# A two-model kernel's prologue: activation table, token sums, a free PSUM bank, order of splits and of one load

## The chip, the cores and the metric

One core of a Trainium2 chip. The metric is the device time of one execution in microseconds (us), the median of several runs. The engines of the core: TensorE (PE: matmuls, PEld: its weight loads), VectorE (DVE), ScalarE (ACT), GpSimd (POOL), and SyncE (SP), which here only issues DMAs. Each engine runs its own program in order and meets the others at semaphores.

## The reference

Two models in a row on 256 tokens of width 1024, in float32. The first has two layers; each normalises x, projects it (pool, attention, indexer, memory attention, gates), lets an indexer pick 64 keys a token, attends to them with a relative bias, attends to 256 memory rows, and merges three gated branches. The second has one layer (a gated delta rule in both directions, a short convolution, a gated feed-forward). The part that matters here is the beginning:

```python
def rms_norm(x, g):
    x32 = x.astype(jnp.float32)
    y = x32 * lax.rsqrt(jnp.mean(x32 * x32, axis=-1, keepdims=True) + EPS)
    return (y * g.astype(jnp.float32)).astype(x.dtype)

# first layer
h = rms_norm(x, norm_g[l])
proj = h @ w_in[l]
mkv = rms_norm(mem, mem_norm_g[l]) @ w_mem_kv[l]
bias = rel_bias[rel_bucket(idx - qpos[None, :, None])]
```

## The kernel before

**Matmuls.** Everything is held with channels on partitions (xT is 128 x 8 x tokens). To keep float32 accuracy, both operands of a product are split into a high part (fp32r) and the low rest, and hi*hi + hi*lo + lo*hi are added in PSUM. The weights come as a stream of blocks of 512 KB (128 x 1024). SP loads block n into raw[slot n % 4] once DVE has split the block four places earlier (`lo_ready`, L422). ACT makes the high half (`split_hi`, L265: waits for the load and for the block four earlier to be done on PE), DVE the low half (`split_lo`, L272). PE then does 24 matmuls of 128 x 256 (`block_cols`, L292: 16 with the high half, 8 with the low), into stream_ps[slot], one PSUM bank a slot; it waits until that bank's last result has been evicted. `ahead(split, engine, G, s)` (L278) splits the block two places behind block s of group G. A group is four blocks.

**The prologue.** Group 0 (blocks 0 to 3) makes iqT and group 1 (blocks 4 to 7) qT of the first layer. They work on u = x * gain, not yet normalised, so that they needn't wait for the token norms; rstd is multiplied in as DVE evicts (`scaled`, L1023). `first_blocks` (L307) does blocks 0 and 1 in steps of one k as the parts of u arrive. Then comes the token sum: ACT squares xT (L571), POOL adds the eight squares (`add_squares`, L384, seven additions in place), PE multiplies by ones (L1620), ACT takes Ln and Exp (`rstd_of`, L369). Then blocks 2 to 7, then a product of rel_bias with a bucket table (L1637, into free_ps[1]) that ACT copies to rel_f (L604) and POOL writes out and reads back as hankel (L433, L435). Then the sums of mem's squares (L1641), and groups 2 to 5, which work on mem_hi and mem_lo of both layers (ACT L576, DVE L1050), their results scaled by mem_rstd. At L656 the first layer proper begins with group G0 + 2 on h_hi and h_lo; behind its first block stands the indexer's product (L1672 to L1679) with ikw_hi, made by ACT (L660) from wik.

**Order by hand.** Each engine's program is written out. ACT issues all loads of constants at its start (L553 to L562), ahead of its first activation. It issues the loads of wik and pool_w at L639 and L642, behind all evictions of the prologue. In ACT's program the two splits of `head` (L588, L589) come behind the squares, the splits of blocks 4 and 5 behind rstd_of, and the copy of rel_f (L604) ahead of the splits of group 2. In DVE's program, `head` (L1028) splits blocks 2 and 3 around evictions that wait for rstd. PE waits for cst before its first matmul (L1612).

Of the kernel before, what the change touches and what calls it, by code (L numbers as in the profile page):

```python
# [9 lines left out]
ACT = mybir.ActivationFunctionType  # L10
# [7 lines left out]
D = 1024  # L18
KT = D // P
S = 256  # L20
# [3 lines left out]
HEADS, HD = 8, 64  # L24
# [8 lines left out]
EPS = 1e-6  # L33
# [3 lines left out]
SLOTS = 4  # L37
# [41 lines left out]
def build(nc, a, out):  # L79

    with ExitStack() as ctx:
# [209 lines left out]

        def block_cols(pe, G, s, free, free_at, r_hi, r_lo, parts=None):  # L292


            pe.wait_ge(hi_ready, 4 * G + s + 1)
            pe.wait_ge(free, free_at)
            ps = stream_ps[s][:, 0:r_hi.shape[-1]]
            for k in range(KT):
                if parts and k % 4 == 0:
                    pe.wait_ge(parts[0], parts[1] + k // 4)  # L300
                with_hi(ps, w_hi[s][:, k, :], r_hi[:, k, :], r_lo[:, k, :], k == 0)
            pe.wait_ge(lo_ready, 4 * G + s + 1 + SLOTS)
            for k in range(KT):
                mm = nc.tensor.matmul(ps, w_lo[s][:, k, :], r_hi[:, k, :], start=False, stop=k == KT - 1)  # L304
            mm.then_inc(blk_done, 1)
# [109 lines left out]
        @block.sync  # L415
        def _(sp):

            first = 8 * LAYERS
            order = list(range(first, first + 8)) + list(range(0, first)) + list(range(first + 8, 4 * a["groups"] + AHEAD))
            for n, at in enumerate(order):  # L420
                s = n % SLOTS
                sp.wait_ge(lo_ready, n + 1)  # L422
                sp.dma_start(raw[:, s, :], a["stream"][at]).then_inc(w_in[s], 16)
            sp.wait_ge(stored, 32)

        @block.gpsimd
        def _(pool):
            nc.gpsimd.memset(eps_col[:, :], EPS).then_inc(consts_ready, 1)

# [121 lines left out]
        def _(act):  # L551
# [9 lines left out]
            act.dma_start(rel_sb[:, :], a["rel_bias"]).then_inc(rel_in, 16)  # L561
            act.dma_start(admit[:, :], a["admit"]).then_inc(admit_in, 16)  # L562
            act.wait_ge(gains_in, 16)
            for k in range(KT):
# [3 lines left out]
                if k in (1, 3):  # L568
                    split_hi(act, 0, k // 2)
            for k in range(KT):  # L570
                nc.scalar.activation(wideS[:, k, :], xS[:, k, :], ACT.Square).then_inc(sq_ready, 1)  # L571

# [20 lines left out]

            act.wait_ge(consts_ready, 1)
            head(0)
            for k in range(KT):
# [6 lines left out]
            act.wait_ge(relf_done, 1)  # L603
            nc.scalar.activation(rel_f[:, :], free_ps[1][0:HEADS, :], ACT.Copy).then_inc(relf_ready, 1)  # L604
            ahead(split_hi, act, 1, 2)
# [28 lines left out]
            for l in range(0, LAYERS):  # L634
                G = G0 + LAYER_GROUPS * l

                if l:
                    act.wait_ge(ikwlo_ready, l)
                act.dma_start(wik[:, :, :], a["wik"][l]).then_inc(wik_in, 16)  # L639
                if l:  # L640
                    act.wait_ge(mixed_done, 2 * l)
                act.dma_start(pool_w[:, :, :], a["pool_w"][l]).then_inc(poolw_in, 16)  # L642
                if l:
                    head(l)
                    for s in range(SLOTS):
                        ahead(split_hi, act, G + 1, s)
                        if s in (1, 3):
                            split_norm_half(l, s // 2)
# [364 lines left out]
        def _(dve):  # L1013
# [8 lines left out]

            def scaled(G, s, dst):  # L1023

                dve.wait_ge(blk_done, 4 * G + s + 1 + SLOTS)
                nc.vector.tensor_tensor(dst, stream_ps[s][:, 0:S], rstd[:, 0:S], ALU.mult).then_inc(dve_evac, 1)

# [31 lines left out]

            head(0)  # L1060
            for s in range(SLOTS):
                ahead(split_lo, dve, 1, s)
                if s in (1, 2):
                    split_mem_lo(0, s - 1)
                scaled(1, s, qT[:, s, :])
            for m in range(LAYERS):
# [543 lines left out]
        def _(pe):  # L1610
            pe.sem_inc(blk_done, SLOTS)
            pe.wait_ge(cst_in, 16)  # L1612

            def head(l):


                Gh, D = head_group(l), DVE_EVACS * l
                first_blocks(pe, Gh, dve_evac, D + 1, u_hi, u_lo, (ulo_ready, KT * l + 1), KT)
                pe.wait_ge(sqsum_ready, l + 1)
                nc.tensor.matmul(free_ps[0][:, 0:S], ones, wideS[:, 0, :], start=True, stop=True).then_inc(ss_ready, 1)  # L1620
                for s in range(AHEAD, SLOTS):
                    block_cols(pe, Gh, s, dve_evac, D + s + 1, u_hi, u_lo)
                for s in range(SLOTS):
                    block_cols(pe, Gh + 1, s, dve_evac, D + 4 + s + 1, u_hi, u_lo)

# [9 lines left out]
            head(0)  # L1635
            pe.wait_ge(rel_in, 32)
            nc.tensor.matmul(free_ps[1][0:HEADS, :], rel_sb[:, :], bucket_hot, start=True, stop=True).then_inc(relf_done, 1)  # L1637
            pe.wait_ge(memsum_ready, 1)
            pe.wait_ge(rstd_ready, 1)
            pe.wait_ge(relf_ready, 1)  # L1640
            nc.tensor.matmul(free_ps[0][:, 0:S], ones, mem_sq[:, 0, :], start=True, stop=True)  # L1641
# [541 lines left out]
```

## Time and profile before

| | |
|---|---|
| median of 3 runs | 1297.45 us (1296.86 to 1300.08) |
| profiled execution | 1302.77 us |
| its span | 1301.0 us |
| PE busy | 1227.4 us (94%) |
| DVE, ACT, POOL busy | 867.6, 632.5, 221.9 us |
| mean granted clock of PE | 0.98 |
| DMA | 196.34 MB, mean 151 GB/s |

The span runs from the first to the last instruction of one profiled execution. Busy time is the union of an engine's instructions; a wait is idle time in front of an instruction, put down to what ended last before it. The granted clock is 1.00 at 2.4 GHz and 0.50 at 1.2 GHz. Engine names with a q (ACTq) are the engine's sequencer, which issues DMAs.

### The profile page before, as it was taken

The numbers are of one execution on the slowest core, as the hardware profiler recorded it, in microseconds if no ns is written. First come the engines' busy times: TensorE is split into PE (matmuls) and PEld (weight loads), VectorE is DVE, ScalarE is ACT, GpSimd is POOL, SyncE is SP. The second block draws the span as 40 slices with busy tenths as digits, with TensorE's granted clock in tenths as the row PEclk, the third lists the DMA queues.
The fourth block names the chain that finished last, engine by engine and source line by source line (L and its number), as shares of the span: only waits on it lengthen the run. The fifth ranks groups of instructions, "written<-read, shape, count | busy, mean of one in ns | idle before, by whom it ended". The sixth has DMA issues, their size and how long they took to land.

```text
span 1301.0 us, 26912 instructions
## 1 busy us (share of the span) xinstructions
PE 1227.4 (94%) x11214; PEld 1187.6 (91%) x11214; DVE 867.6 (67%) x1385; ACT 632.5 (49%) x1022; POOL 221.9 (17%) x244
## 2 busy tenths in 40 slices
PE   5999999999999999998799899999999889999997
PEld 5898998999999989998699899999998889999997
DVE  4754855756868566574588686877877476855554
ACT  6644545543645445535477723333333545644443
POOL 3100150002100510021000062633733001000000
PEclk9999999999999999998899999999999899999999
DMA  6554564445655644455354333323233474566653
GB/s 247 182 166 155 170 188 130 130 140 169 215 168 165 188 141 140 130 167 171 97 173 154 116 103 99 96 85 115 71 94 99 146 224 149 179 194 183 190 195 113
DMA packets 59912, 196.34 MB, mean 151 GB/s; under 512 B 6382, under 2 KB 14088, under 8 KB 59664
## 3 DMA queue, kind: packets, MB, share of 16 engines
q1 hardware_dynamic: 49248, 179.33, 44.7%
q10 hardware_dynamic: 10016, 12.90, 2.9%
q0 software_dynamic: 528, 2.40, 0.7%
q8 instruction: 89, 1.46, 0.5%
q14 instruction: 31, 0.25, 0.1%
HBM read 190.37 MB, written 4.23 MB: 150 GB/s over the span
## 4 chain that ended last, share of the span: by engine, by line
PE 83%; DVE 6%; ACT 4%; issue 3%; DVEq 2%; POOLq 1%; DMA 0%; ACTq 0%
PE stream_ps L289 18%; PE stream_ps L290 17%; PE stream_ps L304 13%; PE stream_ps L283 4%; PE stream_ps L285 3%; PE stream_ps L284 3%; PE free_ps L1948 2%; PE free_ps L1960 2%; DVE w_lo L275 2%; PE stream_ps L1790 2%; PE stream_ps L2035 2%; ACT w_hi L269 1%; PE stream_ps L340 1%; PE stream_ps L345 1%; PE stream_ps L341 1%
## 5 line engine op out<-in xcount | busy, mean ns | idle before, releaser
L275 DVE TENSOR_TENSOR w_lo<-raw,w_hi 128x1024 fp32r<-128x1024 f32 x342 | 428.5, 1262 | 212.4 <-ACT w_hi L269 210.3
L269 ACT ACTIVATE w_hi<-raw 128x1024 fp32r<-128x1024 f32 x342 | 356.6, 1053 | 51.7 <-PE stream_ps L1790 26.2
L289 PE MATMUL stream_ps<-h_hi,w_hi 128*128 128x256 f32 (+1 forms) x1440 | 361.8, 289 | 14.1 <-DVE h_lo L1271 7.1
L290 PE MATMUL stream_ps<-h_lo,w_hi 128*128 128x256 f32 (+1 forms) x1440 | 355.8, 284 | 0.0
L289 PEld LDWEIGHTS stream_ps<-h_hi,w_hi 128*128 128x128 f32 x1440 | 274.6, 191 | 21.1 <-issue 14.6
L290 PEld LDWEIGHTS stream_ps<-h_lo,w_hi 128*128 128x128 f32 x1440 | 275.1, 191 | 0.2
L304 PE MATMUL stream_ps<-h_hi,w_lo 128*128 128x256 f32 (+1 forms) x1376 | 193.0, 283 | 3.0 <-DVE w_lo L275 3.0
L304 PEld LDWEIGHTS stream_ps<-h_hi,w_lo 128*128 128x128 f32 x1376 | 176.8, 189 | 3.4 <-DVE w_lo L275 3.4
L283 PE MATMUL stream_ps<-h_hi,w_hi 128*128 128x256 f32 (+1 forms) x384 | 116.7, 304 | 2.1 <-DVE w_lo L275 2.1
L285 PE MATMUL stream_ps<-h_hi,w_lo 128*128 128x256 f32 (+1 forms) x384 | 108.6, 283 | 0.0
L284 PE MATMUL stream_ps<-h_lo,w_hi 128*128 128x256 f32 (+1 forms) x384 | 108.4, 282 | 0.0
L283 PEld LDWEIGHTS stream_ps<-h_hi,w_hi 128*128 128x128 f32 x384 | 72.4, 189 | 6.0 <-DVE w_lo L275 2.5
L284 PEld LDWEIGHTS stream_ps<-h_lo,w_hi 128*128 128x128 f32 x384 | 72.5, 189 | 0.2
L285 PEld LDWEIGHTS stream_ps<-h_hi,w_lo 128*128 128x128 f32 x384 | 72.2, 188 | 0.0
L529 POOL TENSOR_TENSOR lvl<-lvl,cst 128x256 f32<-128x256 f32 x60 | 56.1, 956 | 65.7 <-DVE lvl L1397 49.3
L887 ACT ACTIVATE n<-free_ps 128x128 f32<-128x128 f32 x50 | 13.9, 277 | 102.2 <-PE free_ps L1948 102.2
L289 PE MATMUL stream_ps<-y_hi,w_hi 128*128 128x256 f32 x192 | 47.7, 282 | 0.0
L290 PE MATMUL stream_ps<-y_lo,w_hi 128*128 128x256 f32 x192 | 47.6, 281 | 0.0
L484 POOL TENSOR_TENSOR wide<-wide,soft 128x512 f32<-128x512 f32 x8 | 15.8, 1977 | 178.9 <-DVE soft L1237 178.9
L1308 DVE SCALAR_TENSOR_TENSOR qkvT<-st_raw,gains,qkvT 128x272 f32<-128x272 f32 x96 | 43.8, 498 | 3.4 <-issue 0.9
L289 PE MATMUL stream_ps<-u_hi,w_hi 128*128 128x256 f32 x128 | 34.7, 304 | 11.8 <-DMA cst<-cst_dram 11.8
L389 POOL TENSOR_TENSOR wide<-wide 128x256 f32<-128x256 f32 x21 | 18.8, 893 | 149.4 <-ACT wide L948 104.3
(368 smaller groups left out, 2288.0 us busy)
## 6 DMA issues: line engine op xcount, KB each, us to landing
raw<-stream_dram SPq DMA_DIRECT2D x342, 512.0 KB, 3.8
gate_spill<-gate_out ACTq DMA_DIRECT2D x16, 128.0 KB, 2.4
decay<-gate_spill POOLq DMA_DIRECT2D x2, 640.0 KB, 7.0
xT<-xT_dram ACTq DMA_DIRECT2D x4, 272.0 KB, 8.0
wik<-wik_dram ACTq DMA_DIRECT2D x2, 544.0 KB, 5.2
mem_raw<-memT_dram ACTq DMA_DIRECT2D x2, 512.0 KB, 9.3
hankel<-rel_scratch POOLq DMA_DIRECT2D x1, 1024.0 KB, 8.3
x_spill<-xT ACTq DMA_DIRECT2D x1, 1024.0 KB, 4.8
```

What stands on the lines that cost most here:

```text
L269: nc.scalar.activation(w_hi[s][:, :, :], raw[:, s, :].rearrange("p (k n) -> p k n", k=KT), ACT.Copy).then_inc(hi_ready, 1)
L275: nc.vector.tensor_tensor(w_lo[s][:, :, :], raw[:, s, :].rearrange("p (k n) -> p k n", k=KT), w_hi[s][:, :, :].bitcast(F32), ALU.subtract) ...
L283: nc.tensor.matmul(ps, l_hi, r_hi, start=first, stop=False)
L284: nc.tensor.matmul(ps, l_hi, r_lo, start=False, stop=False)
L285: return nc.tensor.matmul(ps, l_lo, r_hi, start=False, stop=last)
L289: nc.tensor.matmul(ps, l_hi, r_hi, start=first, stop=False)
L290: nc.tensor.matmul(ps, l_hi, r_lo, start=False, stop=False)
L304: mm = nc.tensor.matmul(ps, w_lo[s][:, k, :], r_hi[:, k, :], start=False, stop=k == KT - 1)
L529: nc.gpsimd.tensor_tensor(lvl[:, lvl_slot(level), hs, :], lvl[:, 0, hs, :], col(5 + level).unsqueeze(1).broadcast_to([P, 4, C]), ALU.mult) ...
L1308: op = nc.vector.scalar_tensor_tensor(out=acc, in0=st_raw[:, m % SLOTS, tap:tap + T], scalar=gains[:, bass.ds(G_CONV + 40 * i + 5 * m + ta ...
L1790: mm = nc.tensor.matmul(ps, w_lo[s][:, 4 * c + k, :], y_hi[:, br, k, :], start=False, stop=k == 3)
L1948: mm = nc.tensor.matmul(packed(bank[half][2][rows, j * 32:(j + 1) * 32]), lvl[rows, lvl_slot(level), 4 * half + j, :], later(xy[rows, half ...
```

## The change

- ACT: right behind its DMA issues it waits for `consts_ready` and makes eps_col from a column of ones (Copy with scale EPS), and drains; POOL writes 1.0 instead of EPS. The high halves of blocks 2 and 3 come ahead of the squares 0 and 4, those of blocks 4 and 5 directly ahead of rstd_of. Behind rstd_of ACT issues the loads of wik and pool_w of layer 0. rel_f is read from free_ps[2].
- SP: the load of block 2 (n == AHEAD) waits until the last part of xT is in.
- DVE: the low halves of blocks 2 to 5 come ahead of the wait for rstd and the four evictions of group 0. The eviction of block 4 reads free_ps[1].
- PE: cst is waited for only ahead of the token sum. The token sum comes behind block 2, and directly behind it the rel product, now into free_ps[2]. Block 4 goes into free_ps[1] and waits for no eviction. The sums of mem wait for block 4's eviction instead of rel_f.

```diff
@@ block_cols
-        def block_cols(pe, G, s, free, free_at, r_hi, r_lo, parts=None):
+        def block_cols(pe, G, s, free, free_at, r_hi, r_lo, parts=None, at=None):
-            ps = stream_ps[s][:, 0:r_hi.shape[-1]]
+            ps = (stream_ps[s] if at is None else at)[:, 0:r_hi.shape[-1]]
@@ SP
                 sp.wait_ge(lo_ready, n + 1)
+                if n == AHEAD:
+                    sp.wait_ge(x_in[3], 16)
@@ POOL
-            nc.gpsimd.memset(eps_col[:, :], EPS).then_inc(consts_ready, 1)
+            nc.gpsimd.memset(eps_col[:, :], 1.0).then_inc(consts_ready, 1)
@@ ACT
+            act.wait_ge(consts_ready, 1)
+            nc.scalar.activation(eps_col[:, :], eps_col[:, :], ACT.Copy, scale=EPS)
+            nc.scalar.drain()
             act.wait_ge(gains_in, 16)
...
             for k in range(KT):
+                if k % 4 == 0:
+                    ahead(split_hi, act, 0, k // 4)
                 nc.scalar.activation(wideS[:, k, :], xS[:, k, :], ACT.Square).then_inc(sq_ready, 1)
...
-            act.wait_ge(consts_ready, 1)
-            head(0)
+            ahead(split_hi, act, 0, 2)
+            ahead(split_hi, act, 0, 3)
+            rstd_of(act, 0, S)
+            act.dma_start(wik[:, :, :], a["wik"][0]).then_inc(wik_in, 16)
+            act.dma_start(pool_w[:, :, :], a["pool_w"][0]).then_inc(poolw_in, 16)
...
-            nc.scalar.activation(rel_f[:, :], free_ps[1][0:HEADS, :], ACT.Copy).then_inc(relf_ready, 1)
+            nc.scalar.activation(rel_f[:, :], free_ps[2][0:HEADS, :], ACT.Copy).then_inc(relf_ready, 1)
@@ DVE
-            head(0)
+            for s in range(SLOTS):
+                ahead(split_lo, dve, 0, s)
+            dve.wait_ge(rstd_ready, 1)
+            for s in range(SLOTS):
+                scaled(0, s, iqT[:, s, :])
             for s in range(SLOTS):
                 ahead(split_lo, dve, 1, s)
                 if s in (1, 2):
                     split_mem_lo(0, s - 1)
-                scaled(1, s, qT[:, s, :])
+                scaled(1, s, qT[:, s, :], None if s else free_ps[1])
@@ PE
-            pe.wait_ge(cst_in, 16)
...
-                pe.wait_ge(sqsum_ready, l + 1)
-                nc.tensor.matmul(free_ps[0][:, 0:S], ones, wideS[:, 0, :], start=True, stop=True).then_inc(ss_ready, 1)
+                if l:
+                    token_sums(l)
                 for s in range(AHEAD, SLOTS):
                     block_cols(pe, Gh, s, dve_evac, D + s + 1, u_hi, u_lo)
+                    if (l, s) == (0, AHEAD):
+                        token_sums(0)
                 for s in range(SLOTS):
-                    block_cols(pe, Gh + 1, s, dve_evac, D + 4 + s + 1, u_hi, u_lo)
+                    if (l, s) == (0, 0):
+                        block_cols(pe, Gh + 1, s, dve_evac, D + 1, u_hi, u_lo, None, free_ps[1])
+                    else:
+                        block_cols(pe, Gh + 1, s, dve_evac, D + 4 + s + 1, u_hi, u_lo)
+
+            def token_sums(l):
+
+                pe.wait_ge(sqsum_ready, l + 1)
+                if l == 0:
+                    pe.wait_ge(cst_in, 16)
+                    pe.wait_ge(rel_in, 32)
+                nc.tensor.matmul(free_ps[0][:, 0:S], ones, wideS[:, 0, :], start=True, stop=True).then_inc(ss_ready, 1)
+                if l == 0:
+                    nc.tensor.matmul(free_ps[2][0:HEADS, :], rel_sb[:, :], bucket_hot, start=True, stop=True).then_inc(relf_done, 1)
...
             head(0)
-            pe.wait_ge(rel_in, 32)
-            nc.tensor.matmul(free_ps[1][0:HEADS, :], rel_sb[:, :], bucket_hot, start=True, stop=True).then_inc(relf_done, 1)
             pe.wait_ge(memsum_ready, 1)
             pe.wait_ge(rstd_ready, 1)
-            pe.wait_ge(relf_ready, 1)
+            pe.wait_ge(dve_evac, SLOTS + 4 + 1)
```

In the ACT program of the layers, the two loads at L639 and L642 are now issued only for layer 1.

## Rows read from the trace of the kernel before

**Rows 1.** Of the page, section 1: busy time, share of the span and instructions by engine.

```profile
PE 1227.4 (94%) x11214; PEld 1187.6 (91%) x11214; DVE 867.6 (67%) x1385; ACT 632.5 (49%) x1022; POOL 221.9 (17%) x244
```

**Rows 2.** The list of waits, PE, 0 to 130 us: total, times, longest.

```profile
PE stream_ps L289 <- DMA cst<-cst_dram: 11.8, 1, 11.8
PE free_ps L289 <- ACT ikw_hi L660: 3.0, 1, 3.0
PE free_ps L1620 <- POOL wide L389: 2.5, 1, 2.5
PE stream_ps L289 <- DVE mem_lo L1050: 1.6, 1, 1.6
PE free_ps L1641 <- ACT rel_f L604: 0.8, 1, 0.8
```

**Rows 3.** Stretches: length, busy us (instructions) PE, PEld, DVE, ACT, POOL; PEclk; DMA share; GB/s.

```profile
11.80:16.93 5.13, 5.13 (x23) 5.00 (x24) 4.08 (x8) 5.13 (x14) 1.98 (x3) 1.00 1.03 405
...
22.67:27.45 4.78, 4.78 (x26) 4.73 (x26) 1.58 (x3) 3.98 (x6) 0.00 (x0) 0.64 0.21 84
...
27.45:41.86 14.41, 14.41 (x123) 14.27 (x122) 8.08 (x12) 7.65 (x19) 7.86 (x7) 1.00 0.45 146
...
47.34:51.06 3.72, 3.71 (x18) 3.72 (x19) 2.95 (x5) 3.51 (x7) 0.00 (x0) 0.54 0.89 307
...
102.56:105.68 3.12, 3.12 (x15) 3.12 (x16) 1.97 (x2) 1.17 (x2) 0.00 (x0) 0.50 0.22 85
```

**Rows 4.** The timeline around PE's start: start us, duration us, engine, line, operation.

```profile
6.20 0.47 ACTq L562 DMA_DIRECT2D admit<-admit_dram  x1
...
7.49 1.28 ACT L394 ACT_TABLE_LOAD   x1 [7.49 <-DMA xT<-xT_dram]
...
8.78 0.91 ACT L394 ACTIVATE u_hi<-xT,gains 128x256 fp32r<-128x256 f32 x2
...
11.34 1.04 ACT L269 ACTIVATE w_hi<-raw 128x1024 fp32r<-128x1024 f32 x1
...
12.43 0.58 PE L289 MATMUL stream_ps<-u_hi,w_hi 128*128 128x256 f32 x1
```

**Rows 5.** The timeline, ACT, PE and DVE, further on.

```profile
25.23 0.42 ACT L374 ACTIVATE rstd<-rstd 128x256 f32<-128x256 f32 x1
...
30.85 3.30 ACT L576 ACTIVATE mem_hi<-mem_raw,gains 128x256 fp32r<-128x256 f32 x8
...
41.86 1.02 PE L1637 MATMUL free_ps<-rel_cst,rel_sb 32*8 32x512 f32 x2
...
42.92 0.59 ACT L604 ACTIVATE rel_f<-free_ps 8x512 f32<-8x512 f32 x1 [7.82 <-PE free_ps L1637]
...
45.63 0.87 DVE L1050 SCALAR_TENSOR_TENSOR mem_lo<-mem_raw,gains,mem_hi 128x256 fp32r<-128x256 f32 x2
```

**Rows 6.** DMA issues, those at 3.11 and at 11.92 us: KB each, us to landing.

```profile
xT<-xT_dram ACTq DMA_DIRECT2D x1, 272.0 KB, 8.3
...
raw<-stream_dram SPq DMA_DIRECT2D x1, 512.0 KB, 5.1
```

**Rows 7.** The timeline, POOL and DVE, while the token squares are added.

```profile
14.67 7.95 POOL L389 TENSOR_TENSOR wide<-wide 128x256 f32<-128x256 f32 x7 [13.83 <-ACT wide L571]
...
17.49 1.73 POOL L389 TENSOR_TENSOR wide<-wide 128x256 f32<-128x256 f32 x1
...
18.55 1.76 DVE L275 TENSOR_TENSOR w_lo<-raw,w_hi 128x1024 fp32r<-128x1024 f32 x1
```

**Rows 8.** The list of waits, PE, whole span, and a stretch behind one of them.

```profile
PE stream_ps L289 <- DVE h_lo L1220: 3.1, 2, 1.6
...
321.00:325.00 4.00, 3.50 (x29) 3.50 (x30) 1.05 (x2) 0.32 (x1) 0.00 (x0) 1.00 0.41 131
```

**Rows 9.** The timeline, ACT, around the indexer's weights.

```profile
97.81 1.07 ACT L269 ACTIVATE w_hi<-raw 128x1024 fp32r<-128x1024 f32 x1
...
101.83 0.68 ACT L660 ACTIVATE ikw_hi<-wik 128x576 fp32r<-128x576 f32 x1 [2.94 <-DMA wik<-wik_dram]
```

More of the change, by code:

```diff
@@ L638, in _ @@
                     act.wait_ge(ikwlo_ready, l)
-                act.dma_start(wik[:, :, :], a["wik"][l]).then_inc(wik_in, 16)
-                if l:
+                    act.dma_start(wik[:, :, :], a["wik"][l]).then_inc(wik_in, 16)
                     act.wait_ge(mixed_done, 2 * l)
-                act.dma_start(pool_w[:, :, :], a["pool_w"][l]).then_inc(poolw_in, 16)
-                if l:
+                    act.dma_start(pool_w[:, :, :], a["pool_w"][l]).then_inc(poolw_in, 16)
                     head(l)
@@ L1021, in _, with scaled @@
                     split_lo(dve, 0, k // 2)
-            def scaled(G, s, dst):
+            def scaled(G, s, dst, at=None):
                 dve.wait_ge(blk_done, 4 * G + s + 1 + SLOTS)
-                nc.vector.tensor_tensor(dst, stream_ps[s][:, 0:S], rstd[:, 0:S], ALU.mult).then_inc(dve_evac, 1)
+                nc.vector.tensor_tensor(dst, (stream_ps[s] if at is None else at)[:, 0:S], rstd[:, 0:S], ALU.mult).then_inc(dve_evac, 1)
             def head(l):
```

## Prediction

> **What bounds the kernel now.** The page comes first: TensorE (PE) is busy 94% of the span of 1301.0 us [rows 1], so time is to be had only where PE stands still or runs at half clock. The list of PE's waits up to 130 us names five, 19.6 us together [rows 2]: 11.8 for the constants (cst), 2.5 for the token squares' sum on GpSimd (POOL), 0.8 for rel_f, 1.6 for the last low part of mem, 3.0 for ikw_hi. The table of stretches puts them in order and adds what they cost behind them [rows 3]. After the 2.5 us wait the granted clock is 0.64, after the mem wait 0.54, after the indexer's wait 0.50; 0.50 is 1.2 GHz, 1.00 is 2.4 GHz. A matmul then takes 0.208 us (3.12 us for 15) where the undisturbed rows of 27.45 to 41.86 give 0.117 (14.41 for 123). So each such spell costs about (0.208-0.117) x 15 = 1.4 us (102.56 to 105.68) to (0.207-0.117) x 18 = 1.6 us (47.34 to 51.06). All edits lie ahead of 106 us; what follows starts after PE and moves with it.
>
> The profiled execution took 1302.77 us, 1.8 more than its span; the three timed runs have a median of 1297.45. I work in differences of the trace and take them off the median.
>
> **A. Table load and start.** The first table load stands between the landing of xT and the first u_hi, 7.49 to 8.77 [rows 4]. Now it comes right behind ACT's last DMA issue, 6.20 + 0.47 = 6.67. Load 1.28, a copy of one column at 0.2 (an estimate, half of the 0.42 for 256 columns in [rows 5]) and a drain: the first u_hi starts at about 8.25 instead of 8.78. It has its data: xT's first part landed by 7.49, and the two loads held back can only make it earlier. ACT then works without a gap, so the second block's high half, ended at 11.34 + 1.04 = 12.38, ends at 11.85. PE, freed of the wait for cst, does one pair of matmuls at about 10.1 and then waits for that half: the start at 11.80 was nearly hidden behind it anyway, since the second block's first matmul came at 12.43 [rows 4]. So taking away the 11.8 us wait is worth the shift alone, 0.5 us: blocks 0 and 1, which had ended 2.5 us ahead of the sums' matmul at 22.67, at 20.14 [rows 2, 3], end at 19.6. Bounds: 0 (the clock rises no earlier than before, at 16.93) and 1.0 (it rises a little earlier relative to the work). The row has 1.28 us from load to next instruction. The Trainium skill (ScalarE: Activation LUTs, What ACT_TABLE_LOAD costs) gives 2.66 us with its drain; by that u_hi would come at 9.5, and A would be -0.7. The trace has u_hi 0.01 us behind the load and disagrees.
>
> **B. Sums behind the third block, fifth block in a free bank.** PE fills the old wait with block 2: 24 matmuls x 0.117 = 2.8 us, 19.6 to 22.4. Its high half needs load 2, which SP now issues only when all of xT is in. The last part of xT landed at 3.11 + 8.3 = 11.4 [rows 6]; the two held loads are 1.05 MB, 2.6 us at 405 GB/s [rows 3], so it lands at about 8.8, load 2 at 8.8 + 5.1 = 13.9 (the time to landing of the next load, [rows 6]) and load 3 some 2 us behind, 15.9. ACT reaches load 2's split at 13.45 and now has the squares behind it: split 2 at 13.9 to 14.95, squares 0 to 3 to 16.1, split 3 to 17.2, squares 4 to 7. PE needs these halves at 19.6 and 22.4: hidden. POOL isn't: its first addition, at 14.67, moves to 15.5.
>
> How long do the seven additions take? They took 7.95 us. One that started while VectorE (DVE) was at w_lo took 1.73 [rows 7]; two such low halves lie in the stretch, and each held POOL up about 0.9 beyond a plain addition's pitch of 0.88 (7 x 0.88 + 2 x 0.9 = 7.95). The new DVE order puts four low halves (blocks 2, 3, 4, 5) ahead of the evictions, and all may fall in this stretch. I take three that hit: 15.5 + 7 x 0.88 + 3 x 0.95 (0.9, or 1.0 at worst) = 24.5. Bounds: one hit, 22.6; four, 25.5; and with xT landing as late as before (11.4, load 2 at 16.5) 27.8. The Trainium skill (GPSIMD Engine Reference, 1. Specifications) has the same rule, that POOL's SBUF interface contends with DVE instructions of two SBUF inputs; the row agrees. Without contention the sums would be ready at 21.7, ahead of block 2's end.
>
> So PE waits at its new place, 22.4 to 24.5, 2.1 us. Behind the waits of 2.5 (token squares), 3.0 (ikw_hi) and even 1.6 us (mem) the clock was halved [rows 2, 3], behind one of 1.6 us (h_lo at 321.5) it stayed at 1.00 [rows 8]; 2.1 lies between the two that lost it, so I count one spell of 1.6. The token sum takes 0.3, the rel product, now behind it, 1.02 [rows 5]. Block 3 starts at 24.5 + 0.3 + 1.0 = 25.8. From block 3's start to the end of the eighth block was 27.45 to 41.86, 14.4 [rows 3]: it ends at 25.8 + 14.4 + 1.6 = 41.8, where before the rel product had ended at 41.86 + 1.02 = 42.9. **A and B together: 1.1 us** (bounds: sums at 22.4 and no spell, 4.8; sums at 27.8 and a spell, -2.2).
>
> The rest of B hides. rstd comes 3.0 us behind the sum (22.67 to 25.65, [rows 3, 5]), at 27.5, while block 3 runs to 30.2. Block 4 goes into free_ps[1], so it waits for no eviction; block 5 needs evictions 0 and 1, done at 28.3, and starts at 33.0. Without the free bank block 4 would still be in time by 2 us.
>
> **C. Between own blocks and mem.** ACT stood 7.82 us on the rel product's result, until 42.92 [rows 5], with the splits of the next blocks behind it; DVE's w_lo and mem_lo hung on these, in its own order, and PE on mem_lo until 47.34 [rows 2, 3]. Now the result is there at 26, so ACT passes. What is late next: with ACT free of rstd at 27.5, squares of mem 2.5, split 1.0, mem_hi 3.3, split 1.0, rel_f 0.6, split of mem's block 0 1.0, at about 37 [rows 4, 5]; DVE, in order, has the second half of mem_lo behind its own halves of that and of the block before, 37 + 2 x 1.2 + 1.7 + an eviction = about 42 [rows 5]. PE wants it at 41.8 + 0.9 (mem's sums) + 1.0 = 43.7. No wait. Saved: 0.77 + 1.64 + 1.6 (spell) = **4.0 us**; the rel product itself was counted in B. Bounds: 4.0, and 2.3 if mem_lo is just late enough to leave 1 us and part of a spell.
>
> **D. Indexer's load.** wik, issued at 96.81 behind the evictions, landed at 101.8, and ikw_hi waited 2.94 for it [rows 9]. PE waited 3.0 [rows 2] and then ran 15 matmuls at half clock. Issued at about 27.5, it lands long before. ACT reaches ikw_hi at 97.81 + 1.07 = 98.9 and ends it at 99.6, when PE's block ends (102.56 less the wait): no wait left. Saved: 2.95 + 1.4 = **4.35 us**; bounds 3.0 (a spell comes all the same) and 4.35. The price: two issues of about 0.5 us (as at 6.20, [rows 4]) behind the Exp, while ACT's engine has work queued, and 0.8 MB on the DMA engines, which carry 84 GB/s around 25 us against 405 when full [rows 3]: nothing.
>
> **Sum:** 1.1 + 4.0 + 4.35 = 9.5 us. 1297.45 - 9.5 = **1287.9**.
>
> **Rivals.**
> 1. The sums come in time (POOL meets only one low half, or the half-clock spell stays out). For it: adding first makes DVE wait instead (w_lo of 1.76 against 1.23, [rows 7]). A and B give 4.8: 13.2 in all, **1284.3**. Chance 0.22.
> 2. The sums come at the late bound, because the held loads do: load 2 at 16.5, ACT standing at it with all squares behind. A and B give -2.2, so 6.2 in all, **1291.3**. The same place is reached if mem_lo stays a wait. Chance 0.20.
> 3. Slower than before: the same in-order chain (SP held for xT, ACT at load 2 and 3, squares, POOL, sums, rstd, evictions) with each us passed on to PE one for one. It decides once the sums come later than 24.5 + 9.5 = 34; at 36 it would be **1299.4**, and over 0.3% slower from 38. Against it: the loads of this stretch took 5 to 8 us to land [rows 6], and these would have to take 10 more. 0.04.
> 4. The change doesn't do what it says: PE stays as long at the indexer's product because ACT's split, not the load, is what ends last. Then D is 0 and the time 1287.9 + 4.35 = **1292.3**. Against it: ACT was free from 98.88 on and named the DMA. 0.04.
> Forecast: 0.50.
>
> **Range.** 1284.3 to 1291.3 are the two neighbours' centres. Further on, PE waits more than once for about 1.6 us [rows 8], a length that cost the clock in one place and not in another; a shifted start may add or take away one spell, 1.5 us. So 1282.5 to 1292.5. About 0.3% (3.9 us) is what a measurement of this kernel can tell from no change: faster by more means under 1293.6. Faster 0.91, within 0.05, slower 0.04.
>
> **What the profile after would show.** A: the table load at 6.7, the second block's first matmul at 11.9. B: PE's wait for POOL now behind three blocks; the third block's rows at 0.12 us pitch; additions of 1.5 to 1.8 us where DVE does w_lo; no PE wait for an eviction. C: no PE row waiting for rel_f or mem_lo, clock 1.00 from 30 to 90 us. D: no PE wait for ikw_hi. Wrong would be: sums before 22.4 or after 28; a wait of mem_lo over 1 us; a time outside the range with all these as said, which would put the cause behind 110 us.

## The result

The changed kernel takes 1291.20 us, the median of six runs (1288.21 to 1293.24), the kernel before, beside it, 1298.59 (1296.86 to 1301.15). The ratio is 0.994, with a 95% interval of 0.9924 to 0.9957: 7.4 us or 0.6% faster. Forecast were 9.5 us.

The profiled execution took 1290.48 us, with a span of 1288.7; from its page:

```profile
PE 1221.3 (95%) x11214; PEld 1181.9 (92%) x11214; DVE 866.9 (67%) x1385; ACT 633.5 (49%) x1023; POOL 221.0 (17%) x244
```

The span is 12.3 us shorter than before's, where the medians differ by 7.4; the first group of experiments takes that apart. PE's waits up to 130 us, which answer [rows 2] (total, times, longest):

```profile
PE stream_ps L289 <- ACT w_hi L269: 11.1, 2, 10.1
PE free_ps L1648 <- POOL wide L389: 2.7, 1, 2.7
```

The first line is the start, 10.1 us for the first block's high half and 1.0 for the second's. Five waits have become this start and one wait of 2.7 for the sums; rel_f, mem_lo and ikw_hi are gone. The stretches that answer [rows 3] (length, busy us of PE, PEld, DVE, ACT, POOL, PEclk, DMA share, GB/s):

```profile
22.40:25.18 2.78, 0.10 (x2) 0.01 (x1) 1.27 (x1) 0.54 (x1) 2.44 (x3) 1.00 0.68 200
...
25.18:30.18 5.00, 5.00 (x20) 3.81 (x21) 1.09 (x3) 4.21 (x10) 1.20 (x2) 0.66 0.73 228
...
39.00:90.00 51.00, 51.00 (x421) 50.53 (x420) 35.99 (x58) 28.32 (x44) 0.74 (x1) 1.00 0.59 193
...
90.00:130.00 40.00, 40.00 (x338) 38.33 (x338) 23.09 (x42) 20.88 (x37) 0.12 (x1) 1.00 0.48 148
```

PE stands from 22.4 to 25.18 with block 2 done, then runs a spell at half clock (0.66 over the stretch, 5 us long), and from 39 to 130 us is never idle at clock 1.00. In the kernel before, [rows 3], that range had a spell of 0.54 and one of 0.50.

### The profile page after: what moved, and what is told of

It is laid out like the page before. It is cut to its first block, busy times and chain, and to the rows that moved or that the text cites. A ratio compares the mean times of both kernels' runs of the same rounds, so it can differ in the third digit from the quotient of the medians.

```text
span 1288.7 us, 26915 instructions
## 1 busy us (share of the span) xinstructions
PE 1221.3 (95%) x11214; PEld 1181.9 (92%) x11214; DVE 866.9 (67%) x1385; ACT 633.5 (49%) x1023; POOL 221.0 (17%) x244
## 4 chain that ended last, share of the span: by engine, by line
PE 83%; DVE 6%; ACT 4%; issue 3%; DVEq 2%; POOLq 1%; ACTq 0%
PE stream_ps L289 18%; PE stream_ps L290 17%; PE stream_ps L304 13%; PE stream_ps L283 4%; PE stream_ps L285 3%; PE stream_ps L284 3%; PE free_ps L1972 2%; PE free_ps L1984 2%; DVE w_lo L275 2%; PE stream_ps L1814 2%; PE stream_ps L2059 2%; ACT w_hi L269 1%; PE stream_ps L340 1%; PE stream_ps L341 1%; PE stream_ps L345 1%
## 5 line engine op out<-in xcount | busy, mean ns | idle before, releaser
L289 PEld LDWEIGHTS stream_ps<-h_hi,w_hi 128*128 128x128 f32 x1440 | 273.3, 190 | 20.8 <-issue 14.6
L895 ACT ACTIVATE n<-free_ps 128x128 f32<-128x128 f32 x50 | 13.9, 278 | 102.2 <-PE free_ps L1972 102.2
L289 PE MATMUL stream_ps<-f_hi,w_hi 128*128 128x256 f32 x176 | 42.8, 281 | 1.5 <-DVE f_lo L1608 1.5
```

Of the source, the lines that this page charges most:

```text
L289: nc.tensor.matmul(ps, l_hi, r_hi, start=first, stop=False)
```

## The experiments

Each kernel is the changed one with one edit, unless said otherwise; the letters A to D are the parts of the prediction. Beside the times, one place of the trace serves as a mark: PE's first large wait behind the prologue, the transposes of layer 0. Where a kernel reaches it tells what the prologue gave, without what happens in the 1100 us behind it. A spell is a stretch of PE at half clock. A single one costs about 1.7 us in these traces (5.00 us at 0.66, above), a double one twice that.

### How much of the difference is the kernel's, and how much the clock's

The first trace of before reaches the mark at 200.43, that of the changed kernel at 191.41 (timeline, PE):

```profile
200.43 0.33 PE L1730 MATMUL free_ps<-cst,soft 128*128 128x128 f32 x1 [2.32 <-DVE soft L1148]
```

```profile
191.41 0.33 PE L1754 MATMUL free_ps<-cst,soft 128*128 128x128 f32 x1 [2.31 <-DVE soft L1160]
```

The changed kernel, unedited, a second time.

> The changed kernel itself, timed again. In the first trace it was 9.0 us ahead of before when both reached the wait of the first layer's transposes (191.41 against 200.43), and 12.3 us ahead at the end, while the timed medians differ by 7.4. Theory: the prologue gives 9 us every time, and what comes on top or is taken away behind it is half-clock spells of PE, some 1.5 us each, that fall in some executions and not in others. Then the median is 7 to 10 us under before, the trace reaches that wait again at 190 to 193, and the half-clock spells behind 200 us are not the same ones as in the first trace. Rival: a steady difference behind 200 us. Then the same spells are missing again and the span is again 12 us shorter.

1292.11 us against 1300.75 for before on the same chip: ratio 0.9925 (0.991 to 0.9941), 8.6 us. Its stretches at the sums, and its timeline at the mark:

```profile
21.80:25.30 3.50, 0.00 (x1) 0.00 (x0) 1.14 (x1) 0.45 (x1) 3.02 (x4) 1.00 0.74 215
...
25.30:32.20 6.90, 6.90 (x23) 4.54 (x23) 1.08 (x3) 5.64 (x13) 2.29 (x4) 0.51 0.56 186
```

```profile
193.12 0.33 PE L1754 MATMUL free_ps<-cst,soft 128*128 128x128 f32 x1 [2.31 <-DVE soft L1160]
```

PE has finished block 2 earlier in this execution (its matmuls of 0.21 us each give way to those of 0.12 at 15.1 us, where the first trace has it at 16.4) and waits 3.5 us; the sums come at 25.3 all the same. The spell behind them is twice as long (6.9 us at 0.51), and the mark comes 1.7 us later, at 193.12, just past the 190 to 193 expected. The spells at the mark and later that the first trace lacked are missing again, as the rival had it. A third time, beside the last group of experiments:

> The changed kernel once more, beside the three below on the same chip. Theory: 7 to 10 us under before, and the first large wait behind the prologue (the transposes of layer 0) is reached between 191.4 and 193.1 again, the 1.7 between them being the length of one half-clock spell at 25 us.

1290.91 against 1300.14: ratio 0.9927 (0.9911 to 0.9944), 9.2 us. Its wait, the stretch behind it, and the mark:

```profile
PE free_ps L1648 <- POOL wide L389: 2.2, 1, 2.2
```

```profile
25.09:30.10 5.01, 5.01 (x33) 3.82 (x34) 1.38 (x4) 4.21 (x10) 1.20 (x2) 1.00 0.80 252
```

```profile
189.82 0.33 PE L1754 MATMUL free_ps<-cst,soft 128*128 128x128 f32 x1 [2.33 <-DVE soft L1160]
```

PE waits 2.2 us for the sums and keeps the full clock. The time is as expected; the mark, at 189.82, lies below the 191.4 to 193.1 that I had expected. So the same program reaches it at 189.8, 191.4 or 193.1, with no spell, a single or a double one behind the same wait. The kernel before, looked at again:

> The kernel before, looked at once more. Theory: the half-clock spells at 201 and 1075 us, which its first trace had and the first two traces of the changed kernel hadn't, come and go from one execution to the next, as do single and double lengths in the prologue. Then this trace lacks at least one of them or has another. Rival: they belong to the kernel; then both are there at the same places.

Its waits, then the stretches behind three of them:

```profile
PE free_ps L1620 <- POOL wide L389: 2.2, 1, 2.2
...
PE stream_ps L289 <- DVE mem_lo L1050: 1.6, 1, 1.6
```

```profile
22.40:27.20 4.80, 4.80 (x39) 4.75 (x40) 1.59 (x3) 4.00 (x6) 0.00 (x0) 1.00 0.17 60
...
45.55:49.30 3.75, 3.75 (x31) 3.75 (x32) 3.75 (x7) 3.54 (x7) 0.00 (x0) 1.00 0.80 269
...
99.37:102.56 3.19, 3.19 (x15) 3.19 (x16) 1.97 (x2) 1.17 (x2) 0.00 (x0) 0.50 0.21 82
```

```profile
197.27 0.33 PE L1730 MATMUL free_ps<-cst,soft 128*128 128x128 f32 x1 [2.31 <-DVE soft L1148]
```

The waits are those of [rows 2], but only the indexer's is followed by half clock. Behind the sums and behind mem_lo the clock stays at 1.00, where the first trace had 0.64 and 0.54 [rows 3]. The mark is at 197.27, 3.2 us ahead of the first trace. With two traces of before (mean 198.9) and three of the changed kernel (mean 191.5) the prologue gives 7.4 us.

How much of this is clock follows from the stretches shown, as an estimate: each costs its length times one minus its clock. Before lost 1.7 + 1.7 + 1.6 = 5.0 us in its first trace [rows 3] and 1.6 in its second, the changed kernel 1.7, 3.4 and 0. Without these the mark is at 195.4 and 195.7 before, and at 189.7, 189.7 and 189.8 after. So 5.8 us of the prologue's gain are waits that are gone or shorter, much the same in all five traces; the other 1.6 are spells, which vary by 3.4 us from one execution to the next in either kernel.

Behind the mark my theory did not hold. Both traces of before take 1100.6 us from the mark to the end, the three of the changed kernel 1097.3, 1097.6 and 1098.0 (spans less marks). The spells at the mark and at 1072, which I expected to come and go, are there in both traces of before, and absent in the first two of the changed kernel, as the rival had it (the third has the later one, not the one at the mark). But it is not code: the kernel without the early table load (below), whose instructions from the mark on are those of the changed kernel, has both, and takes 1099.8. The stretches behind the mark and behind the later wait, of before's second trace, of the changed kernel's first, and of that kernel with its arrival at the mark; then the stretch behind the mark of the changed kernel's second trace:

```profile
198.16:201.57 3.41, 3.41 (x18) 3.41 (x18) 1.41 (x2) 1.76 (x2) 0.00 (x0) 0.50 0.66 233
...
1071.97:1075.38 3.41, 3.41 (x18) 3.41 (x18) 0.00 (x0) 0.00 (x0) 0.00 (x0) 0.50 0.02 5
```

```profile
191.41:194.82 3.41, 3.40 (x29) 3.41 (x30) 1.78 (x2) 1.76 (x2) 0.00 (x0) 1.00 0.68 227
...
1062.83:1066.24 3.41, 3.41 (x29) 3.41 (x30) 1.06 (x1) 0.75 (x1) 0.00 (x0) 1.00 0.02 7
```

```profile
193.05 0.43 PE L1752 MATMUL free_ps<-cst,soft 128*128 128x128 f32 x1 [2.31 <-DVE soft L1158]
...
193.15:196.56 3.41, 3.41 (x17) 3.41 (x18) 1.17 (x2) 1.76 (x2) 0.00 (x0) 0.50 0.79 225
...
1066.96:1070.37 3.41, 3.41 (x19) 3.41 (x18) 0.00 (x0) 0.00 (x0) 0.00 (x0) 0.50 0.02 5
```

```profile
193.12:196.53 3.41, 3.41 (x29) 3.41 (x30) 1.78 (x2) 1.76 (x2) 0.00 (x0) 1.00 0.68 213
```

These two reach the mark 0.07 us apart, at 193.05 and 193.12, behind the same wait of 2.31 us, and one loses the clock and the other keeps it. So the time at which PE arrives doesn't decide it either. What does is not shown by any run.

Added up in stretches of 1 us, each its length times one minus its clock, half clock behind the mark costs 20.8 us in both traces of before and 16.6, 18.3 and 17.4 in the three of the changed kernel. Taken off the 1100.6 and the 1097.3 to 1098.0, this leaves 1079.8 for before and 1079.3 to 1080.7 for the changed kernel: by this estimate the 3 us behind the mark are clock. Over the changed kernel and its nine variants, all with the same instructions there, twelve traces need 1097.3 to 1099.9, so 2.6 us of it come and go; but none reaches the 1100.6 of before.

The timed runs bear this out. Each is on record with its span and its mean granted clock, and span times one minus clock is again an estimate of what half clock cost. On the chip of the second comparison it is 23.8 us in the mean of nine runs of before and 20.1 of five of the changed kernel; on that of the third, 23.6 (eleven runs) and 19.1 (six). The rest of the span is shorter by 5.8 and 4.9 us, near the prologue's 5.8. So of the 7.4, 8.6 and 9.2 us of the three comparisons some 5 to 6 are the waits, and the remainder is half clock that fell less often on the changed kernel, in the prologue and behind it; whether it would stay so after any further edit is open. The 12.3 us between the two first spans have a chance extreme in them: before's profiled execution, 1302.77 us, is slower than each of the six runs timed beside the changed kernel.

### D: the indexer's load

```diff
-            act.dma_start(wik[:, :, :], a["wik"][0]).then_inc(wik_in, 16)
-            act.dma_start(pool_w[:, :, :], a["pool_w"][0]).then_inc(poolw_in, 16)
...
-                    act.dma_start(wik[:, :, :], a["wik"][l]).then_inc(wik_in, 16)
+                act.dma_start(wik[:, :, :], a["wik"][l]).then_inc(wik_in, 16)
...
-                    act.dma_start(pool_w[:, :, :], a["pool_w"][l]).then_inc(poolw_in, 16)
+                act.dma_start(pool_w[:, :, :], a["pool_w"][l]).then_inc(poolw_in, 16)
```

(both loads of layer 0 back at their old place)

> The changed kernel with the loads of wik and pool_w of layer 0 back at their old place. Theory (the prediction's D): PE waits 2.95 us for ikw_hi again and then runs 15 matmuls at half clock; 4.35 us slower than the changed kernel, 3.0 if the clock holds. Rival: the early load is a cost that hides, so the late one costs under 2 us.

1296.12 us, 4.0 above the changed kernel on the same chip (ratio to before 0.9961, 0.9945 to 0.9976). PE's wait, the spell behind it, and the mark:

```profile
PE free_ps L289 <- ACT ikw_hi L668: 3.2, 1, 3.2
```

```profile
100.77:104.20 3.43, 3.43 (x19) 3.43 (x18) 1.22 (x1) 0.18 (x1) 0.00 (x0) 0.51 0.27 68
```

```profile
197.79 0.33 PE L1754 MATMUL free_ps<-cst,soft 128*128 128x128 f32 x1 [2.31 <-DVE soft L1160]
```

3.2 us of wait, a spell of 1.7, and 4.7 us at the mark against the trace of the changed kernel that also had the double spell at the sums (193.12). The theory of D holds. Both traces of before have a spell behind this wait too (0.50). In the changed kernel ACT does ikw_hi right behind its split, without idle time:

```profile
94.19 0.70 ACT L668 ACTIVATE ikw_hi<-wik 128x576 fp32r<-128x576 f32 x1
```

### C: the rel product

```diff
             head(0)
+            nc.tensor.matmul(free_ps[2][0:HEADS, :], rel_sb[:, :], bucket_hot, start=True, stop=True).then_inc(relf_done, 1)
             pe.wait_ge(memsum_ready, 1)
```

(and the same line taken out of token_sums)

> The changed kernel, but the rel product is done behind block 7, as before (its bank and all else as changed). Theory (the prediction's C): ACT stands on its result from about 35.6 to 43 again, with the splits of mem's first blocks behind it; PE waits about 2.4 us in one or two places around 43 to 48 and loses the clock for 1.6. 4.0 us slower than the changed kernel. Rival: the wait was already gone through the other moves (the earlier order of the splits); then under 1 us.

1294.04 us against 1301.97 for before: ratio 0.9943 (0.9925 to 0.996), where the changed kernel had 0.9925 and 0.9927 on other chips. That is 2.1 to 2.3 us slower, with intervals that overlap: neither the 4.0 that was expected nor the under 1 of the rival. The wait and the mark:

```profile
PE stream_ps L289 <- DVE mem_lo L1058: 1.6, 1, 1.6
```

```profile
44.08 0.38 PE L289 MATMUL stream_ps<-mem_hi,w_hi 128*128 128x256 f32 x1 [0.66 <-ACT w_hi L269]
...
195.56 0.33 PE L1753 MATMUL free_ps<-cst,soft 128*128 128x128 f32 x1 [2.31 <-DVE soft L1160]
```

The wait for mem_lo of [rows 2] is back at its 1.6 us, with 0.66 ahead of it for a high half, and in this trace half clock follows (0.52 from 46.92 to 50.50). Against the trace of the changed kernel with the same single spell at the sums (191.41) the mark is 4.15 us later. So C is 2.3 us of waiting, about what the timed runs give, and up to 1.7 more where the clock falls.

### B: the place of the sums, and what makes them late

```diff
-                if l:
-                    token_sums(l)
+                token_sums(l)
                 for s in range(AHEAD, SLOTS):
                     block_cols(pe, Gh, s, dve_evac, D + s + 1, u_hi, u_lo)
-                    if (l, s) == (0, AHEAD):
-                        token_sums(0)
```

> The changed kernel with the token sums and the rel product back ahead of block 2. Theory: the sums come at 25.2 as in the changed kernel, because POOL sets them, and PE, with blocks 2 not yet done, waits 5.5 us for them instead of 2.7: 2.8 us slower, and up to 4.5 with a longer half-clock spell. Rival: POOL is faster with PE idle, or the place of the sums doesn't matter; then under 1.5 us.

1297.53 us, ratio 0.9963 (0.995 to 0.9976): 4.7 to 4.9 us above the changed kernel by the ratios, somewhat more than the 2.8 to 4.5 expected. The list of waits, and the stretch of half clock:

```profile
PE free_ps L1645 <- POOL wide L389: 6.0, 1, 6.0
```

```profile
21.96:32.20 10.24, 7.21 (x24) 4.86 (x25) 2.28 (x3) 4.92 (x12) 5.29 (x7) 0.50 0.55 189
```

6.0 us instead of 2.7, until 25.0 (25.1 to 25.3 in the changed kernel), and the half clock lasts 10 us. So it is the new place that gives POOL 3 us of cover; without it the change would have lost in this stretch, because its other edits make the sums later than before (22.67). Why they are later is told by the changed kernel's timeline of ACT, its row of the DMA issue of block 2's load (us to landing last), and POOL's timeline:

```profile
6.60 1.28 ACT L566 ACT_TABLE_LOAD   x1 [6.60 <-issue]
...
7.90 0.20 ACT L566 ACTIVATE eps_col<-eps_col 128x1 f32<-128x1 f32 x1
...
8.23 0.91 ACT L394 ACTIVATE u_hi<-xT,gains 128x256 fp32r<-128x256 f32 x2
...
14.56 1.06 ACT L269 ACTIVATE w_hi<-raw 128x1024 fp32r<-128x1024 f32 x1 [1.13 <-DMA raw<-stream_dram]
...
15.52 0.70 ACT L578 ACTIVATE wide<-xT 128x256 f32<-128x256 f32 x2
```

```profile
raw<-stream_dram SPq DMA_DIRECT2D x1, 512.0 KB, 5.6
```

```profile
16.31 8.81 POOL L389 TENSOR_TENSOR wide<-wide 128x256 f32<-128x256 f32 x7 [15.47 <-ACT wide L578]
...
21.06 1.53 POOL L389 TENSOR_TENSOR wide<-wide 128x256 f32<-128x256 f32 x1
```

ACT stands 1.13 us for the load of block 2, until 14.56, and splits it before the first square; POOL starts at 16.31 instead of 14.67 and needs 8.81 us instead of 7.95 [rows 7], an addition beside a w_lo of DVE taking 1.53. Three edits take these apart. First the squares ahead of the splits:

```diff
             for k in range(KT):
-                if k % 4 == 0:
-                    ahead(split_hi, act, 0, k // 4)
                 nc.scalar.activation(wideS[:, k, :], xS[:, k, :], ACT.Square).then_inc(sq_ready, 1)
+            ahead(split_hi, act, 0, 0)
+            ahead(split_hi, act, 0, 1)
```

> The changed kernel with ACT's eight squares ahead of the high halves of blocks 2 and 3, DVE's order as changed. It parts the 3.7 us that both reorderings gave together. Theory: the place of the squares is most of it: the first addition starts at 14.1 (2.2 earlier than 16.3), two low halves hold POOL up, the sums come at about 22.3, PE waits under 0.7 us. Then 3 to 3.7 us faster than the changed kernel. Rival: the low halves of blocks 4 and 5, which start at 20.7, now hit the last two additions (+1.7): sums at 23.5, PE waits 1 us and may lose the clock; 1 to 2.5 us faster.

1289.07 us, ratio to before 0.9908 (0.9893 to 0.9922), 2.2 to 2.5 us under the changed kernel by the ratios. POOL's additions and PE's wait:

```profile
14.04 8.79 POOL L389 TENSOR_TENSOR wide<-wide 128x256 f32<-128x256 f32 x7 [13.21 <-ACT wide L576]
```

```profile
PE free_ps L1648 <- POOL wide L389: 0.3, 1, 0.3
```

The additions start at 14.04 and PE waits 0.3 us. The wait is all but gone, as the theory had it; the time gained lies in what was given for the rival. Then the low halves of blocks 4 and 5 behind the first evictions:

```diff
-            for s in range(SLOTS):
-                ahead(split_lo, dve, 0, s)
-            dve.wait_ge(rstd_ready, 1)
-            for s in range(SLOTS):
-                scaled(0, s, iqT[:, s, :])
+            ahead(split_lo, dve, 0, 0)
+            ahead(split_lo, dve, 0, 1)
+            dve.wait_ge(rstd_ready, 1)
+            scaled(0, 0, iqT[:, 0, :])
+            scaled(0, 1, iqT[:, 1, :])
+            for s in (2, 3):
+                ahead(split_lo, dve, 0, s)
+                scaled(0, s, iqT[:, s, :])
```

> The changed kernel with the low halves of blocks 4 and 5 behind the first evictions, as before; the squares stay where the change put them. Theory: two low halves fewer in POOL's way, each worth 0.8: the sums come at 23.5 instead of 25.2, PE waits 1.0 us instead of 2.7, and the half-clock spell goes in some executions: 1.7 to 3.2 us faster than the changed kernel. Rival: PE then misses the low half of block 4; under 1 us faster.

1289.15 us, 1.8 under the changed kernel beside it (ratio to before 0.9912, 0.9894 to 0.9929). Its wait and the stretch behind:

```profile
PE free_ps L1651 <- POOL wide L389: 1.2, 1, 1.2
```

```profile
23.61:28.50 4.89, 4.89 (x32) 3.70 (x33) 1.89 (x4) 4.01 (x9) 1.03 (x1) 1.00 0.49 145
```

1.2 us instead of 2.7, at full clock: the low end of what the theory had. The sums come at 23.6, 1.5 us earlier: two low halves out of POOL's way. Both edits together:

> The changed kernel, but ACT makes all eight squares ahead of the high halves of blocks 2 and 3, and DVE makes the low halves of blocks 4 and 5 behind the first evictions, as before. Theory: PE's 2.7 us wait for the sums at 25.2 is made by the order of ACT's work (the first addition started at 16.3 instead of 14.1, behind the split that stood waiting for the held load) and by low halves of DVE that hold POOL's additions up. Then the first addition starts at about 14.1, the sums come at 22 to 22.7, PE waits under 0.5 us, no half-clock spell follows, and the time is 3.5 to 5 us under the changed kernel. Rival: the sums are late because of POOL alone; then PE still waits over 1.5 us and the gain is under 1.5 us.

1288.43 us, 3.7 under the changed kernel on the same chip and 12.3 under before: ratio 0.9905 (0.9889 to 0.9921). The additions, the sum's matmul with no idle time in front of it, and the mark:

```profile
14.11 8.02 POOL L389 TENSOR_TENSOR wide<-wide 128x256 f32<-128x256 f32 x7 [13.28 <-ACT wide L576]
...
22.42 0.59 PE L1651 MATMUL free_ps<-wide,cst 128*128 128x256 f32 x2
...
187.01 0.44 PE L1757 MATMUL free_ps<-cst,soft 128*128 128x128 f32 x2 [2.30 <-DVE soft L1163]
```

Sums at 22.42, in step with block 2's end, and the mark 187.01, 2.8 us ahead of the changed kernel's earliest trace. This version has the lowest median of all. By the ratios it is hardly faster than the squares alone (0.9905 against 0.9908, on different chips): with these first, PE waited only 0.3 us, so little was left for the low halves to give. Last, the hold on block 2's load:

```diff
-                if n == AHEAD:
-                    sp.wait_ge(x_in[3], 16)
```

> The changed kernel, but SP issues the load of block 2 (and with it block 3) without waiting for xT. Theory: the hold bought nothing, since ACT is the one that paces the start, and it cost ACT 1.1 us of standing at block 2's split (13.43 to 14.56). Then PE's start stays at 10.1 and 11.9, the first addition moves from 16.3 to 15.2, the sums come about 1 us earlier and the time is 0.5 to 2.5 us under the changed kernel (the upper end if the half-clock spell goes with it). Rival: xT then lands late as before (11.4) and PE's start moves back; then the time is 0.5 us or more over it.

1290.19 us, ratio 0.9916 (0.9902 to 0.9929): 1.9 under the changed kernel on the same chip, with intervals that overlap. ACT, POOL and PE's wait:

```profile
8.45 0.91 ACT L394 ACTIVATE u_hi<-xT,gains 128x256 fp32r<-128x256 f32 x2
...
13.55 1.04 ACT L269 ACTIVATE w_hi<-raw 128x1024 fp32r<-128x1024 f32 x1
...
15.29 9.30 POOL L389 TENSOR_TENSOR wide<-wide 128x256 f32<-128x256 f32 x7 [14.45 <-ACT wide L576]
```

```profile
PE free_ps L1646 <- POOL wide L389: 2.2, 1, 2.2
```

The split of block 2 comes at 13.55, with no wait, the additions start 1.0 us earlier and take 0.5 longer, and PE waits 2.2. That is the theory's direction, with 0.5 us at the sums in the trace (24.6 for 25.18) where 1 was expected. The mark is at 190.89, also 0.5 ahead of the trace with the same single spell (191.41); the rest of the 1.9 us isn't explained. So the hold on block 2's load, meant to help the start, gives PE nothing and costs it up to 0.5 us.

### A: the table load, and the free bank

```diff
-            act.wait_ge(consts_ready, 1)
-            nc.scalar.activation(eps_col[:, :], eps_col[:, :], ACT.Copy, scale=EPS)
-            nc.scalar.drain()
```

(and POOL writes EPS again, which ACT waits for ahead of rstd_of)

> The changed kernel without the early activation that brings the table (eps_col is set by POOL as before). Theory: the first u_hi starts 0.5 us later, but ACT stands at block 2's split until its load is in (14.56) either way, so the squares, the sums and PE behind them don't move: within 0.5 us of the changed kernel. Rival (the prediction's A): the 0.5 us goes through to the end.

1290.42 us, 0.5 under the changed kernel beside it (ratio to before 0.9922, 0.9905 to 0.9938): no difference, as the theory had it. But the later start that both theories took for granted doesn't come. ACT's start, and PE's wait:

```profile
6.95 1.28 ACT L394 ACT_TABLE_LOAD   x1 [6.95 <-DMA xT<-xT_dram]
...
8.25 0.51 ACT L394 ACTIVATE u_hi<-xT,gains 128x256 fp32r<-128x256 f32 x1
```

```profile
PE free_ps L1646 <- POOL wide L389: 3.1, 1, 3.1
```

The first u_hi starts at 8.25, against 8.23, 8.08 and 8.16 in the three traces with the early table load. With the loads of blocks 2 and 3 held back, the first part of xT lands earlier, and the table load that follows its landing starts at 6.95 instead of 7.49 [rows 4] or, in before's second trace, 7.21. And without the hold, but with the early table, u_hi starts at 8.45, where before has 8.78 and 8.50. So the hold alone gives the start what both give; both are not worth more. For PE the start hardly counts in either case: what is won there lengthens its wait for the sums. The free bank last (DVE's eviction of block 4 reads stream_ps[0] again, too):

```diff
-                    if (l, s) == (0, 0):
-                        block_cols(pe, Gh + 1, s, dve_evac, D + 1, u_hi, u_lo, None, free_ps[1])
-                    else:
-                        block_cols(pe, Gh + 1, s, dve_evac, D + 4 + s + 1, u_hi, u_lo)
+                    block_cols(pe, Gh + 1, s, dve_evac, D + 4 + s + 1, u_hi, u_lo)
```

> The changed kernel with block 4 in its own bank stream_ps[0], waiting for block 0's eviction. Theory: the eviction (28.6) is done before PE needs the bank (31.4): no wait, the same time within 1 us. Rival: PE waits for it.

1291.33 us, 0.4 over the changed kernel beside it (0.9933, 0.9914 to 0.9951), and no wait of PE but those of the changed kernel. The free bank gives nothing here, as the prediction's 2 us in hand had it.

## Why the prediction was right, and where it was off

- **The sum.** 9.5 us were forecast, of which 3.0 were two spells and 6.5 waits. The waits gave 5.8 at the mark; what is missing is mostly the 0.6 us by which PE waits longer for the sums (2.7 for 2.1). The spells gave 1.6 in the prologue, and up to 3 more behind it, where the forecast had put nothing. That two of the three comparisons come within 1 us of 9.5 is therefore in part luck. In absolute terms the 1291.20 us lie nearer to the second rival's 1291.3 than to the forecast 1287.9, though its mechanism, sums at 27.8, did not come: 1.1 of the 3.3 us are before's median, 1298.59 beside the changed kernel instead of 1297.45, and 2.1 the smaller gain.
- **The places of the waits** came as worked out. The sums were foreseen at 24.5 (bounds 22.6 to 27.8) and came at 25.18, with PE's wait 2.7 instead of 2.1; a spell of half clock followed in two of three traces; no wait of mem_lo, rel_f or ikw_hi; no eviction waited for.
- **The late sums** are step B's own mechanism and the runs confirm both parts of it: ACT's order (2.2 us at the first addition) and POOL held up by DVE's low halves (1.5 us for two, foreseen 0.95 each). What was mis-sized is the first addition, 16.31 instead of 15.5: load 2 took 5.6 us to land instead of 5.1, and a few tenths more went by on the way. The additions themselves took 8.81 us where 7 x 0.88 + 3 x 0.95 = 9.0 were foreseen. The late bound, 27.8, doesn't follow from its terms: load 2 at 16.5 instead of 13.9 moves 24.5 to 27.1.
- **The spells** are the term that was mis-sized. I counted each spell of the one trace of before as certain, 1.6 behind mem_lo among them, and so a gain whenever the wait goes. The second trace of before has no spell behind the sums or mem_lo, and the changed kernel has none, a single or a double one behind the same wait. C was 2.4 + 1.6; the wait is confirmed (0.66 + 1.63), the spell comes in some executions only. And I let all that lies behind 106 us move with PE unchanged; there, half clock came and went too, and differed by 3 us.
- **D** held: 4.35 foreseen, 4.0 by the times and 4.7 at the mark. It is the largest single part of the gain.
- **A**'s times held (u_hi 8.23 against 8.25, second block's first matmul 11.88 against 11.9), its cause did not: the hold alone brings the same start. I had written that the hold "can only make it earlier" and then gave the whole shift to the table. Its lower bound has the clock rise at 16.93: the matmuls do get faster there (23 in 5.13 us ahead of it, one each 0.12 us behind), but the granted clock of that stretch is 1.00 [rows 3], so no row shows a rise of the clock; in the changed kernel the pace changes at 15.1, 16.4 and 17.4. The 2.66 us that the Trainium skill (ScalarE: Activation LUTs, What ACT_TABLE_LOAD costs) gives for a load with its drain doesn't show here either, in the changed kernel: 6.60 + 1.28, and the next activation at 7.90.
- **The rivals.** Sums in time (1284.3) is what the version with both reorderings approaches, 12.3 us under before where the rival had 13.2; it was not the change's case. Late sums at 27.8, the slower case, and the indexer's split as the last to end did not come.

## What to carry to other kernels

Moving a wait behind more work helps only until the thing waited for is itself delayed by the edits beside it: read what runs ahead of the producer on each in-order engine (here ACT's splits ahead of the squares) and what else holds it up (here DVE's splits into low halves, 0.8 us for each on POOL's additions) before reordering. A load that is issued late although nothing it needs is late is cheap to move: issuing wik earlier gave 4 us here. Where the same wait is followed by half clock in some executions and not in others, as those of 1.6 to 2.5 us were here, count the spell as a chance, not as a price, and look at a second trace before taking a difference of two.

## What the runs showed that was not expected

- The same wait of PE, 2.2 to 3.5 us, was followed by no spell, a single and a double one in three executions of one program (1.00, 0.66 and 0.51 in the stretches behind it), worth 3.3 us between the extremes. Two executions that reached a wait of 2.31 us at 193.05 and 193.12 us went on at 0.50 and at 1.00.
- Holding back two 512 KB loads on SP's queue moved the landing of xT's first part, issued earlier on ACT's queue, so that the table load behind it starts at 6.95 instead of 7.49 or 7.21 us. The loads held back had been issued later than that part of xT, and on another queue; they had slowed it by 0.3 to 0.5 us. The four loads of xT take 5.8 us to land in the median in the changed kernel, and 7.8 without the hold.
